# FFN columns in blocks of 2, 3, 3, 3 groups, eight-k-tile down panels behind the next gate panel, and a smaller ring for GpSimd's DMAs

## The reference

```python
hn = rms_norm(h, norm_ffn_g[l])
h = h + (jax.nn.silu(hn @ w_ffn_gate[l]) * (hn @ w_ffn_up[l])) @ w_ffn_down[l]
```

## Time and profile before

| | us |
|---|---|
| median of 3 runs (lowest, highest) | 1277.89 (1277.21, 1278.28) |
| span of the profiled execution | 1275.0 |
| busy: TensorE | 1269.4 |
| busy: VectorE | 1024.6 |
| busy: ScalarE | 743.7 |
| chain that ended last: TensorE's share | 96% |
| DMA moved | 281.83 MB, 221 GB/s |

### The profile page before, as it was taken

One profiled execution on the slowest core, in us unless ns is written; L12 is line 12 of the kernel. 1 busy time (PEld: TensorE's weight loads), 2 busy tenths in 40 slices (PEclk: granted clock), 3 DMA queues, 4 the chain that ended last, 5 costly groups with the idle time before them and its releaser, 6 DMA issues.

```text
span 1275.0 us, 15073 instructions
## 1 busy us (share of the span) xinstructions
PE 1269.4 (100%) x5937; PEld 1045.8 (82%) x5937; DVE 1024.6 (80%) x931; ACT 743.7 (58%) x766; POOL 81.5 (6%) x70
## 2 busy tenths in 40 slices
PE   9999999999999999999999999999999999999999
PEld 7888887777788888888888888888888888888887
DVE  5988777778897566578989887878898888788996
ACT  5766565666665344456656655655565655656653
POOL 1212230000000000001000000000000001000000
PEclk9999999999999999999999999999999999999999
DMA  7976746443675654876786669876877689866874
GB/s 250 313 244 189 228 150 215 151 153 118 198 252 188 220 198 167 309 264 181 233 275 220 202 196 282 261 244 207 259 227 250 183 248 282 255 216 192 284 220 118
DMA packets 137445, 281.83 MB, mean 221 GB/s; under 512 B 5328, under 2 KB 13840, under 8 KB 134304
## 3 DMA queue, kind: packets, MB, share of 16 engines
q1 hardware_dynamic: 130624, 250.37, 55.9%
q0 software_dynamic: 6752, 30.51, 12.8%
HBM read 249.38 MB, written 8.41 MB: 202 GB/s over the span
## 4 chain that ended last, share of the span: by engine, by line
PE 96%; DVE 2%; issue 1%; ACT 0%; POOL 0%; DMA 0%; SPq 0%; DVEq 0%; ACTq 0%
PE bank L2132 23%; PE bank L2137 23%; PE bank L2133 23%; PE bank L2072 7%; PE bank L2073 7%; PE bank L2080 7%; PE bank L2019 1%; DVE u_lo L1622 1%; PE bank L2031 1%; PE bank L2046 1%; PE bank L2290 1%; PE bank L1994 0%; DMA x_rows<-in_x 0%; PE bank L2004 0%; ACT u_hi L1116 0%
## 5 line engine op out<-in xcount | busy, mean ns | idle before, releaser
L1116 ACT ACTIVATE u_hi<-quad 128x2048 fp32r<-128x2048 f32 x229 | 435.5, 1915 | 266.8 <-PE bank L2137 158.1
L1622 DVE TENSOR_TENSOR u_lo<-quad,u_hi 128x2048 fp32r<-128x2048 f32 x224 | 508.9, 2287 | 97.8 <-PE bank L2137 49.3
L2132 PE MATMUL bank<-u_hi,xT_hi 128*128 128x512 f32 x644 | 251.0, 390 | 0.0
L2133 PE MATMUL bank<-u_hi,xT_lo 128*128 128x512 f32 x644 | 250.6, 389 | 0.0
L1384 DVE TENSOR_TENSOR w_lo<-raw,w_hi 128x1024 fp32r<-128x1024 f32 (+1 forms) x104 | 122.2, 1183 | 82.2 <-ACT w_hi L954 80.5
L2137 PE MATMUL bank<-u_lo,xT_hi 128*128 128x512 f32 x696 | 186.3, 389 | 0.0
L954 ACT ACTIVATE w_hi<-raw 128x1024 fp32r<-128x1024 f32 (+1 forms) x104 | 105.6, 1025 | 124.5 <-PE bank L2080 109.4
L2137 PEld LDWEIGHTS bank<-u_lo,xT_hi 128*128 128x128 f32 x696 | 130.6, 188 | 27.4 <-DVE u_lo L1622 0.3
L2132 PEld LDWEIGHTS bank<-u_hi,xT_hi 128*128 128x128 f32 x644 | 120.9, 188 | 25.3 <-issue 0.3
L2133 PEld LDWEIGHTS bank<-u_hi,xT_lo 128*128 128x128 f32 x644 | 120.9, 188 | 25.0
L2072 PE MATMUL bank<-w_hi,xT_hi 128*128 128x512 f32 (+1 forms) x256 | 99.4, 392 | 0.0
(11 more groups left out here) (267 smaller groups left out, 1827.1 us busy)
## 6 DMA issues: line engine op xcount, KB each, us to landing
quad<-in_w_ffn_gate SPq DMA_DIRECT2D x44, 1024.0 KB, 7.2
quad<-in_w_ffn_up SPq DMA_DIRECT2D x44, 1024.0 KB, 5.8
quad<-in_w_ffn_down SPq DMA_DIRECT2D x44, 1024.0 KB, 6.5
quad<-in_w_in SPq DMA_DIRECT2D x33, 1024.0 KB, 6.8
raw<-in_w_in SPq DMA_DIRECT2D x24, 1024.0 KB, 5.5
quad<-quad POOLq DMA_DIRECT2D x22, 1024.0 KB, 8.2
raw<-in_w_out SPq DMA_DIRECT2D x12, 1024.0 KB, 5.2
raw<-in_w_branch_b SPq DMA_DIRECT2D x8, 1024.0 KB, 5.6
```

The costliest lines, as they stand in the source:

```text
L1116: A(st.hi[u.hi][:], st.quad[slot][:], ACT.Copy).then_inc(hi_ready, u.step)
L1622: V.tensor_tensor(st.lo[u.lo][:], st.quad[u.panel.slot[u.raw]][:], st.hi[u.hi][:].bitcast(F32), ALU.subtract).then_inc(lo_ready, u.step)
L2132: M(sums, a_hi(k), hi[:, w], start=start and k == 0, stop=False, skip_group_check=True)
L2133: M(sums, a_lo(k), hi[:, w], start=False, stop=False, skip_group_check=True)
```

## The change

The blocks become 2, 3, 3 and 3 groups. With two groups the down panels have eight k-tiles, and so no N units: seven M units and seven products. They are put behind the first gu panel of the next block (here called gu2), whose N2 and N3 then stand in the first of them. The sequence of panels is gu0, gu1, gu2, down, down (8 k-tiles each), gu3, gu4, down, down (12 each), gu5, gu6, gu7, down, down, gu8, gu9, gu10, down, down: 19 panels and 165 + 2 x 7 + 6 x 11 = 245 products. In the text below, D0 and D1 are the two down panels of eight k-tiles.

`fT_hi` and `fT_lo` are used as a ring of four groups. The forms of the block that gu2 begins are made after its second group, with its first difference built from `fT_hi + fT_lo` (two more VectorE operations). `evac` has two buffers of its own instead of one shared with `side_a`, so that ScalarE's waits for the adding DMAs are changed or dropped.

```diff
-FF_BLOCKS = 4
+FF_BLOCKS = (2, 3, 3, 3)
+FF_RING = 4
+DMA_RING = 2048
...
-    down = 0
-    for block, ff in enumerate(range(0, ff_cols, FF_BLOCKS)):
-        k = min(FF_BLOCKS, ff_cols - ff)
-        for i in range(k):
-            p = panel("gu", ff + i, kt)
-            p.block, p.block_slot = block, i
+    starts = [sum(FF_BLOCKS[:block]) for block in range(len(FF_BLOCKS))]
+    down = made = 0
+    for block, (ff, k) in enumerate(zip(starts, FF_BLOCKS)):
+        ahead = 1 if k * GROUP == 2 * UNIT_KT else 0
+        while made < ff + k + ahead:
+            of = max(b for b, start in enumerate(starts) if start <= made)
+            p = panel("gu", made, kt)
+            p.block, p.block_slot = of, made - starts[of]
+            p.forms_late = of > 0 and FF_BLOCKS[of - 1] * GROUP == 2 * UNIT_KT
+            made += 1
         for m in range(d_cols // 2):
             p = panel("down", m, k * GROUP)
-            p.block, p.row, p.down = block, ff * GROUP, down
+            p.block, p.row, p.down, p.first_col = block, ff * GROUP, down, ff
...
-        evac = at("evac", [P, T, COLS], F32, o_stage)
+        evac = [sb(f"evac{half}", [P, T, COLS]) for half in range(2)]
...
-                if t == 0:
-                    if half:
-                        act.wait_ge(out_added0, 16 * (panel.down + 1))
-                    elif panel.prev.kind == "down":
-                        act.wait_ge(out_added1, 16 * panel.down)
-                    else:
-                        act.wait_ge(turned, SETS + panel.prev.col + 1)
+                if t == 0 and panel.down:
+                    act.wait_ge((out_added0, out_added1)[half], 16 * panel.down)
...
-                    if u.name == "N2" and not own:
+                    if u.name == "N2" and not own or u.name == "M1" and not before.has_rest:
                         evacuate(before, 0, 0)
...
                 if panel.block_slot == 1:
+                    if panel.forms_late:
+                        f11 = groups(ring(panel.col - 1)), tokens(0)
+                        dve.wait_ge(fT_ready, hidden_turned(panel))
+                        in_order(V.tensor_tensor(by_group(fs[:, 2, :]), fT_hi[:, f11[0], f11[1]].bitcast(F32),
+                                                 fT_lo[:, f11[0], f11[1]].bitcast(F32), ALU.add))
+                        in_order(V.tensor_tensor(by_group(fs[:, 2, :]), by_group(fs[:, 2, :]), f21, ALU.subtract))
...
-                if u.name == ("M4" if panel.prev.kind == "gu" and "N1" not in panel.unit else "M3"):
+                if u.name == ("M4" if "N1" not in panel.unit and (gu or not panel.has_rest) else "M3"):
                     seed_e(panel)
...
-    nc = bacc.Bacc("TRN2", target_bir_lowering=False, num_devices=1)
+    nc = bacc.Bacc("TRN2", target_bir_lowering=False, num_devices=1, dynamic_dma_scratch_size=DMA_RING)
```

More of the change, by code:

```diff
@@ L156, in __init__ @@
         self.block = self.block_slot = self.row = self.down = 0
+        self.first_col, self.forms_late = 0, False
         self.unit, self.order = {}, []
@@ L172, in add_products, with has_rest @@
                 self.add_unit(name, name, (2 + i) * UNIT_KT)
+    @property
+    def has_rest(self):
+        return self.kts > 2 * UNIT_KT
     def index(self, *names):
@@ L264, in panel @@
         return panels[-1]
-    down = 0
-    for block, ff in enumerate(range(0, ff_cols, FF_BLOCKS)):
-        k = min(FF_BLOCKS, ff_cols - ff)
-        for i in range(k):
-            p = panel("gu", ff + i, kt)
-            p.block, p.block_slot = block, i
+    assert sum(FF_BLOCKS) == ff_cols
+    starts = [sum(FF_BLOCKS[:block]) for block in range(len(FF_BLOCKS))]
[8 more added lines that the diff above has]
+            made += 1
         for m in range(d_cols // 2):
             p = panel("down", m, k * GROUP)
-            p.block, p.row, p.down = block, ff * GROUP, down
+            p.block, p.row, p.down, p.first_col = block, ff * GROUP, down, ff
             down += 1
@@ L679, in rows_before, with ring @@
         def rows_before(panel):
-            return panel.n - len(branches)
+            return len([p for p in heads + panels if p.n < panel.n and p.has_rest])
+        def ring(col):
+            return col % FF_RING
         def a_bank(panel):
@@ L921, in add_out @@
                 pool.wait_ge(evacuated, T * (panel.down + 1))
-                pool.dma_start(out_view[:, :, cs], evac[:], accum_op=ALU.add).then_inc(added, 16)
+                pool.dma_start(out_view[:, :, cs], evac[half][:], accum_op=ALU.add).then_inc(added, 16)
             for panel in panels:
@@ L1258, in gate_opened @@
                         act.wait_ge(turned, SETS + panel.col)
-                    if panel.block and panel.block_slot == 0:
-                        act.wait_ge(out_added1, 16 * downs_before(panel))
                 else:
@@ L1265, in evacuate @@
             def evacuate(panel, half, t):
-                if t == 0:
-                    if half:
-                        act.wait_ge(out_added0, 16 * (panel.down + 1))
-                    elif panel.prev.kind == "down":
-                        act.wait_ge(out_added1, 16 * panel.down)
-                    else:
-                        act.wait_ge(turned, SETS + panel.prev.col + 1)
+                if t == 0 and panel.down:
+                    act.wait_ge((out_added0, out_added1)[half], 16 * panel.down)
                 if half:
                     act.wait_ge(piece_used, panel.c_done + 1)
+                    if t:
+                        act.wait_ge(e_seeded, panel.n + 1)
                 elif t:
                     act.wait_ge(piece_used, panel.b_done + 1)
+                elif panel.has_rest:
+                    act.wait_ge(a_summed, rows_before(panel) + 1)
                 else:
-                    act.wait_ge(a_summed, rows_before(panel) + 1)
+                    act.wait_ge(piece_used, panel.a_done + 1)
                 which = ((a_bank, b_bank), (c_bank, e_bank))[half][t]
-                A(evac[:, t, :], which(panel)[:], ACT.Copy).then_inc((evacuated0, evacuated1)[half], 1)
+                A(evac[half][:, t, :], which(panel)[:], ACT.Copy).then_inc((evacuated0, evacuated1)[half], 1)
             def copy_m1(panel):
@@ L1302, in hidden_hi @@
                 for t in range(1 if panel.block_slot == 0 else T):
-                    A(fT_hi[:, groups(panel.block_slot), tokens(t)], by_group(bank[T_BANK + t][:]),
+                    A(fT_hi[:, groups(ring(panel.col)), tokens(t)], by_group(bank[T_BANK + t][:]),
                       ACT.Copy).then_inc(rows_hi, 1)
@@ L1863, in hidden_lo @@
                     dve.wait_ge(f21_ready, panel.block + 1)
-                    in_order(V.tensor_tensor(by_group(fs[:, 2, :]), by_group(top[0]), f21, ALU.subtract))
+                    if not panel.forms_late:
+                        in_order(V.tensor_tensor(by_group(fs[:, 2, :]), by_group(top[0]), f21, ALU.subtract))
                 if panel.block_slot == 1:
+                    if panel.forms_late:
[4 more added lines that the diff above has]
+                        in_order(V.tensor_tensor(by_group(fs[:, 2, :]), by_group(fs[:, 2, :]), f21, ALU.subtract))
                     V.tensor_tensor(by_group(fs[:, 0, :]), f21, by_group(top[1]), ALU.subtract)
@@ L1869, in hidden_lo @@
                 for t in range(1 if first else T):
-                    V.tensor_tensor(fT_lo[:, groups(panel.block_slot), tokens(t)], by_group(top[t]),
-                                    fT_hi[:, groups(panel.block_slot), tokens(t)].bitcast(F32),
+                    V.tensor_tensor(fT_lo[:, groups(ring(panel.col)), tokens(t)], by_group(top[t]),
+                                    fT_hi[:, groups(ring(panel.col)), tokens(t)].bitcast(F32),
                                     ALU.subtract).then_inc(fT_ready, 1)
@@ L2144, in own @@
             def own(panel, kt0, t):
+                if panel.kind == "down":
+                    kt0 = ring(panel.first_col + kt0 // GROUP) * GROUP
                 return rows_of(flhs[panel.kind][0:2], kt0, t)
```

## The result

The changed kernel takes 1293.24 us in the median of three runs (1293.12 to 1294.41), the kernel before 1277.89: the ratio is 1.0125 with a 95% interval of 1.0112 to 1.0139, so 15.35 us slower. The forecast was 1291.7 us. The profiled execution of the changed kernel took 1293.24 us, with a span of 1291.4.

The account below looks back on a forecast made before the run. TensorE bounds the kernel before; in the 17 M units without N units VectorE becomes late. -5.4 + 16.1 + 3.1 = +13.8 us takes the span from 1275.0 to 1288.8, plus 2.9 gives 1291.7 us; range 1282 to 1297.5.

Parts of the forecast that it names:

- The gain: TensorE's queue: 247 products become 245, 2 x 2.72 us, so 5.44 us less.
- The chain from D0 to gu3: 17 M units without an N unit: VectorE's work and ScalarE round trips make TensorE stall 16.1 us in all.
- 3.76 us for M6 and 3.59 for M7: Stalls of TensorE at M6 and at M7, claimed in D1 and again in gu3.
- The 1.01 us at M5 of gu3: TensorE's stall at M5 of gu3, behind sum P and its round trip: 1.01 us.
- Panels of 12 k-tiles: Second down panels of blocks 1 and 2 stall 0.24 us each, gu5 and gu8 1.3 each: together 3.1 us.
- Rival 4: TensorE's clock falls to 1.2 GHz at the last long stall, behind M7 of gu3: +5.4, 1297.1 us; 6%.
- the time around the span: Whole kernel: the median of the runs lies 2.9 us over the span.
- 1 (no round trips): D0 to gu3: high halves of M5 and M6 hide, only VectorE's sum counts: change +4.4, 1282.3 us; 7%.
- 2 (faster): Same 17 units: VectorE's lead carries the row, two products are pure gain: -5.4, 1272.5 us; 6%.
- 3 (descriptors): Smaller descriptor room holds back weight sums in D1 and gu3: +7.6 on the forecast, 1299.3 us; 6%.
- One cover: Weight sum by DMA, worked out for D1: usual landing 8.2 us, at most 11.6; covered by at least 1.1 us.

Follow-up runs that it names:

- experiment 2: Changed kernel with sums P, R and Z left out in D1 and gu3 (VectorE adds 8 columns into scratch instead): 1284.86 us, ratio 1.0055.
- experiment 3: Changed kernel with M5 and M6 of D1 and gu3 split from tile 22 as loaded, sums still made but not waited for: 1288.51 us, ratio 1.0084.
- experiment 4: Changed kernel plus two 1.224 us VectorE additions behind Z: in D1 and gu3 (dense kernel) 1300.28 us; in gu6 and gu9, a second kernel, 1293.96 us.
- experiment 5: Changed kernel with TensorE turning the identity 20 times before M6 and 16 before M7 of D1 and gu3 while it waits: 1291.47 us, ratio 1.0106.
- experiment 1: Changed kernel with the old blocks of 4, 4 and 3 groups, its other edits kept: 1277.78 us, ratio 1.0001 against the kernel before.
- experiment 7: Changed kernel with order M1, M5, M2, M6, M7 in D1 and gu3, and Z, seed_c, seed_e and some loads moved: 1287.74 us, ratio 1.0078.
- experiment 9: Changed kernel reordered M1, M5, M2, M6, M7, D1's output adds issued in gu4, 2 and 9 identity turns before M5 and M7 of D1 and gu3: 1287.33 us.

## Why the prediction was right, point by point

**The gain**, two products less: 24 matmuls, 5.4 us, as forecast.

**The chain from D0 to gu3** (forecast 16.1 us). On the forecast's clock M6 of D0 starts at 760.98 and M7 of gu3 at 821.51, 60.53 us later. In the trace they start at 719.93 and 780.41, 60.48 us, where plain products would take 44.44: 16.0 us lost. VectorE's steps came as laid out: P to low M5 4.27, R to low M6 4.26, `seed_c` to M7 0.84. Experiments 2, 3 and 4 show that the cause is the one named: its work, and its round trips.

**How it divides** came out a little otherwise. The forecast had 3.76 us for M6 and 3.59 for M7. In the trace the waits are shorter (2.93 and 2.27 in D1) and the products longer (4.45 for M6 with the slow clock). The sum up to M7 is the same, because VectorE sets it. The 1.01 us at M5 of gu3 did not appear, as D1's M7 and M3 had run slowly and TensorE came later.

**Panels of 12 k-tiles** (forecast 3.1 us). In gu5 TensorE needs 3.96 us from M2 to M7, in gu8 too: 1.24 us each, against 1.26 worked out (1.3 in the sum). The second down panels lose 0.27 and 0.24 us, against 0.24. Together 3.0.

**What was left out: the clock.** This is the term that was mis-sized. Rival 4 had it with a chance of 6% and 5.4 us; it did happen, and behind the last gap it cost 4.11 + 3.08 - 2 x 2.72 = 1.75 us. About 0.1 us of that is no clock: M7 of gu5, behind a wait and at the full clock, takes 2.84 us too. Experiment 5 gets 1.8 us back. The chance was too low, since I took it that gaps of 3 us might pass without a fall. Some do (3.38 us in experiment 3), but four of four in the changed kernel did not; the price was too high, since the lower level lasted for a part of two products and not for two whole ones.

**The sum measured**: -5.4 + 16.0 + 3.0 + 1.75 = 15.3, against 15.35 between the medians. The spans differ by 16.4; 0.6 of that lies ahead of the FFN's first turn (599.59 and 600.23 us), in code that is the same in both. Of the 0.5 us that is left over the sum, some 0.4 is in four M7 that stand behind a `seed_c` that came late, in the panels of 12 k-tiles and in gu5 and gu8: they take 2.83 or 2.84 us instead of 2.72. That the forecast time is only 1.5 us off is in part luck: its span of 1288.8 was 2.6 us short, and the time around the span, for which it added 2.9 us, is 1.8. It had taken the 2.9 from a median and the span of one execution.

**The rivals.** 1 (no round trips) and 2 (faster) fall with experiments 3 and 4. 3 (descriptors): experiment 1 shows no cost with the old blocks, and in the changed kernel no wait of GpSimd for room appears; the new blocks with the full room were not run. One cover was near the thin end of what I said: the weight sum by DMA in gu3 lands after 11 us, not 8.2, so it was next in line. In the changed kernel ScalarE waits for it once:

```profile
ACT u_hi L1131 <- DMA quad<-quad: 0.9, 1, 0.9
```

VectorE's low half of M7 is not held up by that, but the DMA took away part of what experiments 2, 3 and 7 should have brought, and my expectations for 2 and 7 had missed that.

## What to carry to other kernels

Saving work on the busiest engine pays only where the engine that feeds it has a lead: an average load of 85% hid panels where the feeder needs 23.3 us for every 19.0. Lay the two queues side by side for the densest stretch, and count each round trip to a third engine at its full start-to-start time. When a feeder becomes the bound, moving one operation ahead in its queue mostly moves the wait; ask at once which transfer is next in line.

## What the runs showed of the hardware

- In the changed kernel the four waits of TensorE of 2.3 to 2.9 us were each followed by a fall of the granted clock (0.84 over ten microseconds), which began 0.8 to 1.5 us into the next product, with a matmul every 0.43 us instead of 0.23. After the wait of 1.09 us in gu5 the products took 2.84 and 2.72 us.
- The length of the wait alone doesn't tell: in experiment 3 a wait of 3.38 us passed at a clock of 1.00 (M7 of D1 took 2.84 us), and in the dense kernel of experiment 4 one of 2.69 us did (before M6 of gu3).
- 20 and 16 turns of the identity in the waiting time kept the clock at 1.00 in all four places and all four executions; with 2 and 9 turns (experiment 9) it was 0.999 or more in two executions and 0.997 in the two others.
- An accumulating DMA of 1 MB from SBUF to SBUF took 8.2 us in the median of the kernel before, and 10.3 to 11.4 us in gu3 of the changed kernel and its variants, with loads of 1 MB and an add of 512 KB under way.
- The room for descriptors of GpSimd's DMAs cut from 16384 to 2048 bytes a partition: a ratio of 1.0001.
